# Prompt attention: gate over denominator applied while the exponentials are turned, in place of a spread, a multiply and two adds

## What is computed

```python
p_c = masked_softmax(s_c, ...)      # compressed blocks, up to 32 keys
p_s = masked_softmax(s_s, ...)      # selected blocks; for this prompt length, all causal keys
p_w = masked_softmax(s_w, ...)      # window of 512 keys
return gc[..., 0:1] * o_c + gc[..., 1:2] * o_s + gc[..., 2:3] * o_w      # o_x = p_x times values
```

## Time and profile before

| | |
|---|---|
| time, median of 3 runs (lowest, highest) | 2065.01 us (2064.51, 2066.19) |
| the profiled execution's own time | 2064.16 us |
| its span, first to last instruction | 2062.5 us |
| mean granted clock of TensorE | 0.962 |
| prompt attention's main block | 286 to 573 us of the span |

### The profile page before, as it was taken

One profiled execution on the slowest core, in us unless ns is written; L12 is line 12 of the kernel. 1 busy time (PEld: TensorE's weight loads), 2 busy tenths in 40 slices (PEclk: granted clock), 3 DMA queues, 4 the chain that ended last, 5 costly groups with the idle time before them and its releaser, 6 DMA issues.

```text
span 2062.5 us, 38066 instructions
## 1 busy us (share of the span) xinstructions
PE 1938.3 (94%) x15625; PEld 1760.9 (85%) x15625; DVE 870.4 (42%) x1702; ACT 585.1 (28%) x1203; POOL 149.7 (7%) x213
## 2 busy tenths in 40 slices
PE   6899969999986899879999999999999999999999
PEld 4668656676673789769999999999999999999998
DVE  6233025666603177633223334644244424442443
ACT  5133135665512124332212222221112111111121
POOL 4000001100030043310000000000000000000000
PEclk8899958999998899989999999999999999999999
DMA  8422553000066310233221122111111111111112
GB/s 238 70 71 64 223 123 119 7 2 2 2 202 231 105 34 24 55 75 83 77 77 49 36 83 82 52 41 41 51 51 43 41 54 46 51 39 53 41 51 85
DMA packets 164891, 148.18 MB, mean 72 GB/s; under 512 B 7769, under 2 KB 152138, under 8 KB 163698
## 3 DMA queue, kind: packets, MB, share of 16 engines
q1 hardware_dynamic: 156852, 126.39, 20.5%
q0 software_dynamic: 6208, 17.67, 3.4%
q10 hardware_dynamic: 1696, 2.22, 0.4%
HBM read 120.54 MB, written 29.99 MB: 73 GB/s over the span
## 4 chain that ended last, share of the span: by engine, by line
PE 54%; DMA 0%; DVE 0%; ACT 0%; issue 0%; SPq 0%; DVEq 0%
PE psum L246 18%; PE psum L247 18%; PE psum L248 18%; DMA state_rows<-in_state_conv 0%; PE psum L850 0%; DMA out_y_prompt<-ys 0%; PE psum L745 0%; PE psum L840 0%; PE psum L800 0%; DVE ys L725 0%; DVE hl L688 0%; DVE hid L684 0%; DVE t_wl L580 0%; ACT hh L518 0%; DVE conv_state L576 0%
## 5 line engine op out<-in xcount | busy, mean ns | idle before, releaser
L247 PE MATMUL psum<-xgl,t_wh 128*128 128x344 f32 x1056 | 338.2, 320 | 0.0
L246 PE MATMUL psum<-xgh,t_wh 128*128 128x344 f32 x1056 | 338.0, 320 | 0.0
L248 PE MATMUL psum<-xgh,t_wl 128*128 128x344 f32 x1056 | 337.3, 319 | 0.0
L247 PEld LDWEIGHTS psum<-xgl,t_wh 128*128 128x128 f32 x1056 | 198.6, 188 | 0.1
L248 PEld LDWEIGHTS psum<-xgh,t_wl 128*128 128x128 f32 x1056 | 198.4, 188 | 0.0
L246 PEld LDWEIGHTS psum<-xgh,t_wh 128*128 128x128 f32 x1056 | 198.2, 188 | 0.1
L246 PE MATMUL psum<-hh,t_wh 128*128 128x344 f32 (+2 forms) x456 | 146.3, 321 | 2.0 <-DVEq L686 1.7
L248 PE MATMUL psum<-hh,t_wl 128*128 128x344 f32 (+2 forms) x456 | 145.9, 320 | 0.0
L247 PE MATMUL psum<-hl,t_wh 128*128 128x344 f32 (+2 forms) x456 | 145.8, 320 | 0.0
L246 PE MATMUL psum<-wh_n,xh 128*128 128x512 f32 (+3 forms) x288 | 112.7, 391 | 18.6 <-DVE wl_n L962 18.6
L580 DVE TENSOR_TENSOR t_wl<-t_raw,t_wh 128x1024 fp32r<-128x1024 f32 (+1 forms) x93 | 112.9, 1214 | 33.7 <-ACT t_wh L499 28.6
(11 more groups left out here) (445 smaller groups left out, 3921.6 us busy)
## 6 DMA issues: line engine op xcount, KB each, us to landing
t_raw<-in_w_gate SPq DMA_DIRECT2D x22, 512.0 KB, 3.8
t_raw<-in_w_up SPq DMA_DIRECT2D x22, 512.0 KB, 3.8
t_raw<-in_w_down SPq DMA_DIRECT2D x24, 384.0 KB, 3.3
cmp_pages<-in_cache_kv SPq DMA_DIRECT2D x64, 128.0 KB, 2.2
t_raw<-in_w_in SPq DMA_DIRECT2D x16, 512.0 KB, 4.0
raw_n<-in_w_in SPq DMA_DIRECT2D x24, 256.0 KB, 3.8
r_raw<-in_w_in SPq DMA_DIRECT2D x12, 512.0 KB, 3.9
xh_copy<-xh SPq DMA_DIRECT2D x1, 4128.0 KB, 13.5
```

The lines of the kernel that those rows point to most:

```text
L246: pe.matmul(out, wh, xh, start=(first and k == 0), stop=False)
L247: pe.matmul(out, wh, xl, start=False, stop=False)
L248: mm = pe.matmul(out, wl, xh, start=False, stop=(last and k == n - 1))
```

## The change

The spread, the multiply and the two adds go. DVE takes the reciprocal of each branch's denominators on its own as soon as its order allows (`inverse`). POOL multiplies the identity by that reciprocal and by the gate, both one number for each partition, into a 128x128 diagonal matrix for each branch and group: six for each unit (`diag`). `turn` becomes an ordinary matmul of the exponentials (weights) by the diagonal (moving), which turns and scales at once, and waits for the diagonals (semaphore `dg`) instead of the exponentials. `values` adds all tiles of a unit into one 128-column region, and `combine` is a copy of that to the output by DVE.

On DVE the reciprocals stand as follows. Those for chunks with exponentials inside a unit's steps come in the same step, behind its copy and reductions. Those for chunks whose exponentials come behind all steps (the window from qt 1 on, all in qt 0) come ahead of the next unit's first copy if their tiles begin in its first group (qt 0 to 2), else behind its first copy and reductions.

```diff
@@ -2016,15 +2016,13 @@
...
     pt = c.low("pt", [P, 2, 8 * P])
-    rsb = c.low("rsb", [P, 2, 3 * P])
-    tmp = c.low("o_tmp", [P, 2, 3 * P])
+    diag = c.low("diag", [P, 2, 3, GROUPS, P])
     lows = c.low("lows", [P, 2, 2, 4])
...
     rec = c.low("rec", [P, 2, 2, 3])
-    sc = c.low("sc", [P, 2, 2, 3])
     zero = c.low("zero", [P, 1])
     NU = 8 * R
-    S = {x: c.sem("a_" + x) for x in ("init", "qk", "red", "ex", "tp", "ev_a", "ev_v", "pv", "rc", "gt", "om", "oa", "ev_r", "sp")}
+    S = {x: c.sem("a_" + x) for x in ("init", "qk", "red", "ex", "tp", "ev_a", "ev_v", "pv", "dg", "ov", "rc")}
     SB, TB, OB = 0, 4, 6
@@ -2044,6 +2042,10 @@
...
         return [tiles[i:i + 8] for i in range(0, len(tiles), 8)]
+    def starts_in(u, kind):
+        return [i for i, gr in enumerate(groups(u)) if any(x[0] == kind[0] for x in gr)][0]
     def pieces(u, i, bank):
@@ -2083,18 +2085,13 @@
...
             in_turn += [(u + 1, kind) for kind in at.get(i, [])]
-            if i == n - 1:
-                in_turn.append((u, "spread"))
     place = {x: n for n, x in enumerate(in_turn)}
...
     def bank_turn(eng, n):
...
             u, kind = in_turn[n - 2]
-            if kind == "spread":
-                eng.wait_ge(S["ev_r"], u + 1)
-            else:
-                eng.wait_ge(S["red"], reds[chunk_no(u, kind)])
+            eng.wait_ge(S["red"], reds[chunk_no(u, kind)])
@@ -2140,45 +2137,36 @@
...
                 for x, (kind, k, g) in enumerate(gr):
-                    pe.wait_ge(S["ex"], 6 * u + exps[{"s": "sel", "w": "win", "c": "cmp"}[kind]])
+                    pe.wait_ge(S["dg"], 6 * u + exps[{"s": "sel", "w": "win", "c": "cmp"}[kind]])
                     if kind == "s":
...
                         at, m = s_c[:, u % 2, g, 0:ncmp], ncmp
-                    mm = pe.transpose(c.psum[0:m, TB + x // 4, (x % 4) * P:(x % 4 + 1) * P], at, c.ident[:, :])
+                    by = diag[:, u % 2, {"c": 0, "s": 1, "w": 2}[kind], g, :]
+                    mm = pe.matmul(c.psum[0:m, TB + x // 4, (x % 4) * P:(x % 4 + 1) * P], at, by, start=True, stop=True)
                     if x == 3 and len(gr) > 4:
...
                 mm.then_inc(S["tp"], 1)
-            def spread(u):
-                n = place[u, "spread"]
-                bank_turn(pe, n)
-                pe.wait_ge(S["gt"], u + 1)
-                for b in range(3):
-                    for g in range(GROUPS):
-                        mm = pe.matmul(c.psum[g * HD:(g + 1) * HD, SB + 2 * (n % 2), b * P:(b + 1) * P],
-                                       sc[:, u % 2, g, b:b + 1].to_broadcast([P, HD]), c.ident[:, :], start=True, stop=True)
-                mm.then_inc(S["sp"], 1)
             def values(u, i):
...
                 if i == 0 and u >= 2:
-                    pe.wait_ge(S["om"], u - 1)
+                    pe.wait_ge(S["ov"], u - 1)
                 wait_evacuated(pe, G)
...
                     if kind == "s":
-                        v, m, b, last = c.v_sel[:, k, lo], P, 1, k == qt
+                        v, m = c.v_sel[:, k, lo], P
                     elif kind == "w":
-                        v, m, b, last = c.v_win[:, k0 + k, lo], P, 2, k == nw - 1
+                        v, m = c.v_win[:, k0 + k, lo], P
                     else:
-                        v, m, b, last = cv[0:ncmp, 0, lo], ncmp, 0, True
-                    mm = pe.matmul(c.psum[lo, OB + u % 2, b * P:(b + 1) * P], v, pt[0:m, G % 2, x * P:(x + 1) * P],
-                                   start=(kind == "s" and k == 0), stop=last, skip_group_check=True)
+                        v, m = cv[0:ncmp, 0, lo], ncmp
+                    mm = pe.matmul(c.psum[lo, OB + u % 2, 0:P], v, pt[0:m, G % 2, x * P:(x + 1) * P],
+                                   start=(kind == "s" and k == 0), stop=(kind == "c"), skip_group_check=True)
                 mm.then_inc(S["pv"], 1)
@@ -2189,8 +2177,6 @@
...
                         score(u + 1, kind)
-                    if i == n - 1:
-                        spread(u)
                     if i:
@@ -2238,17 +2224,6 @@
...
-            def weights(u):
-                qt, r = divmod(u, R)
-                q = u % 2
-                dve.wait_ge(S["ex"], 6 * u + 6)
-                if u >= 2:
-                    dve.wait_ge(S["sp"], u - 1)
-                dve.reciprocal(rec[:, q], den[:, q]).then_inc(S["rc"], 1)
-                dve.wait_ge(S["rc"], u + 1)
-                gate = c.gates[:, qt, :].rearrange("p (g r b) -> p r g b", g=GROUPS, r=R)[:, r]
-                dve.tensor_tensor(sc[:, q], rec[:, q], gate, ALU.mult).then_inc(S["gt"], 1)
             def evac(u, i):
@@ -2258,12 +2233,15 @@
...
+            def inverse(u, kind):
+                b, n = {"sel": (1, 2), "cmp": (0, 4), "win": (2, 6)}[kind]
+                dve.wait_ge(S["ex"], 6 * u + n)
+                dve.reciprocal(rec[:, u % 2, :, b], den[:, u % 2, :, b]).then_inc(S["rc"], 1)
             def combine(u):
-                dve.wait_ge(S["ev_r"], u + 1)
+                qt, r = divmod(u, R)
                 dve.wait_ge(S["pv"], first_group[u + 1])
-                if u >= 2:
-                    dve.wait_ge(S["oa"], 2 * (u - 1))
-                dve.tensor_tensor(tmp[:, u % 2, :], rsb[:, u % 2, :], c.psum[:, OB + u % 2, 0:3 * P], ALU.mult).then_inc(S["om"], 1)
+                dve.tensor_copy(c.o_nsa[:, r, qt * P:(qt + 1) * P], c.psum[:, OB + u % 2, 0:P]).then_inc(S["ov"], 1)
@@ -2273,11 +2251,18 @@
...
                 n, at, later = steps(u)
-                weights(u)
+                last = steps(u - 1)[2].get(len(groups(u - 1)), []) if u else chunks(0)
+                soon = max([x + 1 for x, kind in enumerate(last) if starts_in(u, kind) == 0], default=0)
+                for kind in last[:soon]:
+                    inverse(u, kind)
                 for i in range(n):
...
                         reduced(u + 1, kind)
+                    for kind in last[soon:] if i == 0 else []:
+                        inverse(u, kind)
+                    for kind in later.get(i, []):
+                        inverse(u + 1, kind)
                     if i == 0 and u:
@@ -2289,6 +2274,8 @@
...
                 done = reds[chunk_no(u, kind)]
+                if u >= 2:
+                    act.wait_ge(S["dg"], 6 * (u - 1))
                 for g in range(GROUPS):
@@ -2301,13 +2288,6 @@
...
                     act.activation(pt[0:m, G % 2, x * P:(x + n) * P], c.psum[0:m, TB, x * P:(x + n) * P], ACT.Copy).then_inc(S["ev_a"], 1)
-            def evac_spread(u):
-                n = place[u, "spread"]
-                act.wait_ge(S["sp"], u + 1)
-                if u >= 2:
-                    act.wait_ge(S["om"], u - 1)
-                act.activation(rsb[:, u % 2, :], c.psum[:, SB + 2 * (n % 2), 0:3 * P], ACT.Copy).then_inc(S["ev_r"], 1)
@@ -2318,7 +2298,6 @@
...
                         expo(u + 1, kind)
-                evac_spread(u)
                 for kind in later.get(n, []):
@@ -2337,12 +2316,16 @@
         def _(pool):
...
                 qt, r = divmod(u, R)
-                o = c.o_nsa[:, r, qt * P:(qt + 1) * P]
-                t = tmp[:, u % 2, :]
-                pool.wait_ge(S["om"], u + 1)
-                pool.tensor_tensor(t[:, 0:P], t[:, 0:P], t[:, P:2 * P], ALU.add).then_inc(S["oa"], 1)
-                pool.wait_ge(S["oa"], 2 * u + 1)
-                pool.tensor_tensor(o, t[:, 0:P], t[:, 2 * P:3 * P], ALU.add).then_inc(S["oa"], 1)
+                if u == 0:
+                    pool.wait_ge(S["init"], 2)
+                if u >= 2:
+                    pool.wait_ge(S["tp"], turned[first_group[u - 1]])
+                for j, (kind, b) in enumerate((("sel", 1), ("cmp", 0), ("win", 2))):
+                    pool.wait_ge(S["rc"], 3 * u + j + 1)
+                    for g in range(GROUPS):
+                        at = (g * R + r) * 3 + b
+                        pool.tensor_scalar(diag[:, u % 2, b, g, :], c.ident[:, :], rec[:, u % 2, g, b:b + 1],
+                                           c.gates[:, qt, at:at + 1], ALU.mult, ALU.mult).then_inc(S["dg"], 1)
     c.base = low0
```

## The result

| | before | after |
|---|---|---|
| time, median (lowest, highest) | 2065.54 us (2064.51, 2066.19), 4 runs | 2162.14 us (2158.03, 2163.08), 4 runs |
| the profiled execution's own time, its span | 2064.16, 2062.5 us | 2162.11, 2160.5 us |
| mean granted clock | 0.962 | 0.956 |

The changed kernel takes 1.0464 times as long, 95% interval 1.0446 to 1.0482: slower by 96.6 us, where +63 was forecast and the range ended at 2150.

The account below looks back on a forecast made before the run. TensorE was taken to bound query tiles 3 to 7, a chain of latencies query tile 0. Terms 37.7 + 16.8 + 12 - 2 - 1 = +63.5 us gave 2128 us, range 2098 to 2150 (some 85%).

Parts of the forecast that it names:

- qt 0: Query tile 0: exponentials start some 2 us sooner, chain and dearer tiles eat most; -2 us for four units, bounds -8 and +3.
- the waits of qt 3 to 6: Query tiles 3 to 6: TensorE waits for the window's diagonals 1.8, 1.3, 0.8, 0.3 us a unit; +16.8 us, bounds 0 and 30.
- The turned tile: Turning exponentials by f32 matmul takes two passes, not one: 0.11 us more a tile, +51.9 us in query tiles 3 to 7.
- The rule of four times: Skill's transpose mode 4x faster for FP32: sum some 90 us larger; as rival, four passes for one, 2218 us, 2%.
- The spread's term: Query tiles 3 to 7: the spread goes from TensorE, 0.71 us a unit in 20 units, -14.2 us.
- my rival on the clock: Until about query tile 1: more matmul work brings 2.4 GHz back sooner, 8 us allowed, 2120 us; 7%.
- qt 1 and 2: Query tiles 1 and 2: reciprocal, two diagonals and dearer tiles behind the window's exponentials, some +1.5 us a unit, +12 us.
- The diagonal on POOL: Each diagonal made by POOL takes 0.38 us, bounds 0.23 and 1.0; six a unit, POOL no bound.
- Dear diagonals: Rival: each POOL diagonal takes 1.0 us, +35 us in the 28 units whose window waits, 2163 us; 9%.

Follow-up runs that it names:

- plain turns: The kernel before, with its transposes made ordinary f32 matmuls by the identity and nothing else changed: 2131.6 us, ratio 1.0318.
- window first: The changed kernel, with DVE taking the window's reciprocal ahead of the unit's first copy from query tile 3 on too: 2137.1 us, ratio 1.0344.
- the filler: The changed kernel, with six matmuls nobody reads ahead of the waiting turn in each unit of query tile 3: 2155.0 us, ratio 1.0418.
- three orders: The changed kernel, window's reciprocal ahead of the first copy, diagonals made by DVE, query tile 0's reciprocals ahead of the previous output copy: 2125.8 us, ratio 1.0275.
- scaled in place: As three orders, but exponentials scaled in SBUF (DVE in query tiles 0 and 1, then POOL), turned by transposes, no diagonals: 2081.1 us, ratio 1.0068.
- split groups: As scaled in place, but DVE scales group 0 and POOL group 1 of every branch: 2059.4 us, ratio 0.9966.
- split, then DVE: As split groups in query tiles 0 to 2, but DVE scales both groups from query tile 3 on: 2086.8 us, ratio 1.0094.

## Why the prediction came out as it did

The sign and the main term held. What is left of the forecast besides tiles (592 x 0.11 = 65.1) and spread (-22.7) is 21.1 us, for waits and their order; measured it is 96.6 - 65.6 + 22.7 = 53.7. That group of terms is what failed, and the range did not reach that far. Two of its steps carry most of it: qt 0, 12.4 us over its term, and the waits of qt 3 to 6 with the clock that fell behind them, 8.1 us over theirs.

**The turned tile: right.** 0.11 us was forecast, 65.6 / 592 = 0.11 measured in plain turns. The rule of four times, weighed and set aside, would have added some 90 us to that kernel by the forecast's working; the row of qt 7 has twice. A detail: in qt 3 to 7 of plain turns the price is 56.0 / 472 = 0.12, as in the row of qt 7 ((1.98 - 1.03) / 8), that is 4 us over my 51.9; qt 0 to 2 paid less. The rows count records; that one record is one pass of the array is my reading of them. The spread's term held too: window first, which has neither spread nor waits from qt 3 on, is 13.2 us shorter there than plain turns (239.6 against 252.8), and 14.2 was forecast.

**The new wait, qt 3 to 6: right in its length, wrong in what it left out.** I forecast 1.8, 1.3, 0.8 and 0.3 us a unit, 16.8 in all. TensorE's waits for POOL in those tiles are 8.3, 4.6, 1.6 and 1.2 us, 15.7. But window first, where only the place of the window's reciprocal differs, has no such wait there and gives back 24.9 us in qt 3 to 7 (264.5 against 239.6), most of the rest in qt 3 (13.2 us for 8.3 of waits) and qt 4 (7.2 for 4.6), the two tiles whose granted clock fell. By the clock, 0.10 of 51.9 us and 0.03 of 53.0 are 6.8 of the 9.2 us that the waits cost beyond their length; the other 2.4 are not accounted for. This is one of the two steps that failed: my rival on the clock let it only gain. "From 347 on the clock is 1.00 anyway" was a fact of a kernel whose TensorE never stood still; I planned 1.8 us of standing still in each unit and left the clock at 1.00. The Trainium skill (TensorE: Matmul & The Clock Gate, HAM oscillation — how this bites in real kernels) describes a kernel in which the wait between bursts of matmuls brings the clock down each time; the filler agrees, as six matmuls put into each wait of qt 3 gave back 4.9 us over its four units.

**qt 0: wrong, -2 forecast, +10.4 measured, the largest miss.** I counted what ACT no longer waits for, and one reciprocal and two diagonals of chain; the other two reciprocals of a unit I had costed at nothing. The order on DVE gives six diagonals in a row instead, as shown: the text of the change had it (in qt 0 all reciprocals come behind all steps), and I did not write out POOL's queue for that tile. Some 3 us of it are the diagonals' price and handover (47.1 to 44.1 with DVE; 46.1 and 46.4 in the two other kernels with this code), 4.7 us the order (44.1 to 39.4). The dearer turns alone cost 0.5 in plain turns, where the clock rose. The remaining 2.7 of three orders over before are not pulled apart: its chain still has a wait more, at a clock of 0.56. Some of every part may be clock, 0.51 in after against 0.59 before, for which the forecast has nothing.

**qt 1 and 2: +15.9 against +12**, in its bounds of 4 to 16, but not by its mechanism. I forecast two diagonals behind the window's exponentials; it is six in all eight units, and TensorE's wait of 10.4 us in these tiles stands ahead of the selected tiles, which I had costed at nothing.

**The diagonal on POOL: 0.447 us, 0.38 forecast**, nearer to the tensor_tensor of the earlier trace rows than to the line I drew. Two of them in each of 28 waiting units are 4 us, in the sums above. Dear diagonals lost on its price; its time of 2163 was nearly met, by luck, through another mechanism. The clock rival lost on its sign in this kernel. Its mechanism was not empty: plain turns, with more matmul work and no new waits, was granted 0.74 and 1.00 in qt 0 and 1; after, with its waits, had 0.51 and 0.95.

**The sum, in order.** qt 3 to 7 +67.7 for 54.5, qt 1 and 2 +15.9 for 12, qt 0 +10.4 for -2: 94.0 in the stage for 64.5. The rest of the 98 us between the two profiled executions lies outside: the stage begins 3.6 us later (289.7 against 286.1), and the starts of the other kernels here, of the same code up to there, spread from 286.2 to 290.9. So nothing shows it to be an effect of the change. No row here says what it is; that stays open.

## What to carry to other kernels

A step that goes through TensorE twice as ordinary f32 costs 0.11 us more for each 128-column tile: before folding a scaling into a transpose, count the tiles (592) against the small operations it saves (32 spreads). A scaling of exponentials was cheaper on DVE and POOL side by side (0.9966) than in the matmul, even with the matmul's waits put in order (three orders, 1.0275). When a change puts a new producer on a chain, write out that engine's queue for each kind of tile, not for the typical one: the six in a row of qt 0, and DVE's copy behind its scaling in qt 7, both stood in the order and in no mean. And price a stall on a busy TensorE above its length when the granted clock can fall behind it: in qt 3 it was 13.2 us for 8.3, in qt 5, where the clock stayed at 1.00, 2.6 for 1.6.

## What the runs showed of the hardware

**The clock can fall behind short waits.** TensorE busy for 84% of a stretch, with one wait of 1.6 to 2.3 us in each unit, was granted 0.90 (after, qt 3); with the waits partly filled by matmuls that nobody reads, 1.00.

**POOL beside DVE.** POOL's scaling by two numbers of each partition takes longer when DVE does the same at the same time. Groups by shape, first of scaled in place (POOL alone), then of split groups (both engines):

```profile
L2103 POOL TENSOR_SCALAR s_win<-s_win,rec,gates 128x640 f32<-128x640 f32 x32 | 27.7, 874 | 7.9 <-DVE rec L2252 7.8
L2103 POOL TENSOR_SCALAR s_sel<-s_sel,rec,gates 128x1024 f32<-128x1024 f32 x8 | 9.5, 1197 | 27.8 <-DVE rec L2252 27.8
```

```profile
L2112 POOL TENSOR_SCALAR s_win<-s_win,rec,gates 128x640 f32<-128x640 f32 x16 | 19.4, 1214 | 14.2 <-DVE rec L2256 14.2
L2112 DVE TENSOR_SCALAR s_win<-s_win,rec,gates 128x640 f32<-128x640 f32 x16 | 9.8, 612 | 0.6
L2112 POOL TENSOR_SCALAR s_sel<-s_sel,rec,gates 128x1024 f32<-128x1024 f32 x4 | 7.0, 1741 | 27.9 <-DVE rec L2256 27.9
...
L2112 DVE TENSOR_SCALAR s_sel<-s_sel,rec,gates 128x1024 f32<-128x1024 f32 x4 | 3.3, 814 | 0.1
```

A pair of qt 2 in the timeline of split groups:

```profile
348.17 0.48 DVE L2112 TENSOR_SCALAR s_sel<-s_sel,rec,gates 128x384 f32<-128x384 f32 x1
348.24 0.87 POOL L2112 TENSOR_SCALAR s_sel<-s_sel,rec,gates 128x384 f32<-128x384 f32 x1 [4.64 <-DVE rec L2256]
```

POOL begins 0.07 us behind DVE. If its data pass waits for DVE's end, and 0.23 of its own time (a POOL operation of 8 columns) can lie beside that, 640 columns take (0.612 - 0.07) + (0.874 - 0.23) = 1.19, measured 1.21; 1024 columns (0.814 - 0.07) + (1.197 - 0.23) = 1.71, measured 1.74. The Trainium skill (SBUF — State Buffer, Who interferes with whom) says that DVE and GpSimd share one pair of ports under an exclusive lock; the durations agree. The split does not scale a pair sooner: two of 1024 on DVE take 1.54 us (timeline of split, then DVE), the split pair 0.07 + 1.74. What it gains, by this reading, is that DVE is free for its copies after 0.81. That the lock is the cause was not tried by itself.
